# A hybrid decoder step: value chunks projected last, first head turned inside the last chunk, search opening in nine steps

## Time and profile before

| | before |
|---|---|
| median of three runs | 1811.48 us |
| profiled execution | 1811.48 us, its span 1810.0 us |
| PE busy | 1616.5 us, 89% of the span |
| DVE busy | 873.3 us, 48% |
| ACT busy | 679.2 us, 38% |
| POOL busy | 576.2 us, 32% |
| late projections, search, end of front | 218.9 to 535.5 us of the span |

### The profile page before, as it was taken

One profiled execution on the slowest core, in us unless ns is written; L12 is line 12 of the kernel. 1 busy time (PEld: TensorE's weight loads), 2 busy tenths in 40 slices (PEclk: granted clock), 3 DMA queues, 4 the chain that ended last, 5 costly groups with the idle time before them and its releaser, 6 DMA issues.

```text
span 1810.0 us, 29717 instructions
## 1 busy us (share of the span) xinstructions
PE 1616.5 (89%) x10786; PEld 1514.5 (84%) x10786; DVE 873.3 (48%) x1998; ACT 679.2 (38%) x1777; POOL 576.2 (32%) x715
## 2 busy tenths in 40 slices
PE   4696869899948889887699799999999999999998
PEld 3594669899847777775499699999999999999998
DVE  1904877877857888886521722312313303313214
ACT  4414647757427777874312421021121111111111
POOL 2344145624654343312112052142132232232310
PEclk7798989999979999998799999999999999999999
DMA  7700023353323121103530121111111111111002
GB/s 256 252 24 6 24 89 106 104 186 110 107 83 113 59 94 53 42 8 110 214 118 13 47 84 38 42 46 46 46 46 46 46 46 37 56 46 35 12 1 97
DMA packets 138045, 135.30 MB, mean 75 GB/s; under 512 B 7229, under 2 KB 126957, under 8 KB 137302
## 3 DMA queue, kind: packets, MB, share of 16 engines
q1 hardware_dynamic: 111190, 106.43, 18.4%
q10 hardware_dynamic: 25104, 24.64, 4.2%
q0 software_dynamic: 1648, 2.89, 0.5%
HBM read 115.29 MB, written 27.04 MB: 79 GB/s over the span
## 4 chain that ended last, share of the span: by engine, by line
PE 48%; DVE 2%; ACT 1%; DMA 1%; POOL 0%; issue 0%; DVEq 0%; SPq 0%; ACTq 0%
PE bank L2385 28%; PE wide L2401 14%; PE bank L2364 5%; PE wide L2348 1%; DVE xn L2616 0%; DVE alo L2626 0%; DVE rstd L2600 0%; DMA out_y_p<-yn 0%; DMA ow<-in_w_out 0%; ACT ahi L2501 0%; POOL owl L2532 0%; DVE yn L2670 0%; ACT gwh L2459 0%; PE bank L2425 0%; ACT L2473 0%; ACT L2491 0%
## 5 line engine op out<-in xcount | busy, mean ns | idle before, releaser
L2637 DVE TENSOR_TENSOR hf<-bank,sg 128x352 f32<-128x352 f32 x66 | 34.6, 525 | 464.6 <-PE bank L2385 455.4
L2546 POOL TENSOR_TENSOR hlo<-hf,hhi 128x352 fp32r<-128x352 f32 x66 | 62.6, 949 | 504.9 <-ACT hhi L2475 504.9
L2385 PE MATMUL bank<-ahi,gwh 128*128 128x352 f32 x1056 | 196.5, 328 | 11.2 <-DVE hf L2637 6.6
L2650 DVE SCALAR_TENSOR_TENSOR x<-wide,modT,x 128x352 f32<-128x352 f32 (+1 forms) x264 | 151.3, 573 | 96.8 <-PE wide L2401 96.8
L2385 PE MATMUL bank<-ahi,gwl 128*128 128x352 f32 x1056 | 194.1, 326 | 0.0
L2385 PE MATMUL bank<-alo,gwh 128*128 128x352 f32 x1056 | 192.2, 324 | 2.0 <-DVE alo L2626 2.0
L2385 PEld LDWEIGHTS bank<-ahi,gwh 128*128 128x128 f32 x1056 | 176.3, 190 | 14.1 <-DVE hf L2637 6.9
L2385 PEld LDWEIGHTS bank<-alo,gwh 128*128 128x128 f32 x1056 | 174.4, 189 | 2.7 <-DVE alo L2626 2.7
L2385 PEld LDWEIGHTS bank<-ahi,gwl 128*128 128x128 f32 x1056 | 176.6, 191 | 0.0
L2401 PE MATMUL wide<-hlo,dwh 128*128 128x352 f32 x528 | 171.3, 325 | 0.0
L2401 PE MATMUL wide<-hhi,dwl 128*128 128x352 f32 x528 | 170.4, 323 | 0.0
(11 more groups left out here) (347 smaller groups left out, 3473.1 us busy)
## 6 DMA issues: line engine op xcount, KB each, us to landing
gw<-in_w_gate_up SPq DMA_DIRECT2D x44, 512.0 KB, 4.9
raw<-in_w_ada ACTq DMA_DIRECT2D x14, 1024.0 KB, 8.6
dw<-in_w_down SPq DMA_DIRECT2D x22, 512.0 KB, 3.5
raw<-in_w_ada SPq DMA_DIRECT2D x10, 1024.0 KB, 7.5
raw<-in_w_in ACTq DMA_DIRECT2D x8, 1024.0 KB, 5.8
scr_x<-xT SPq DMA_DIRECT2D x1, 4224.0 KB, 18.3
xnat<-in_x_prompt SPq DMA_DIRECT2D x8, 512.0 KB, 5.3
scr_q<-ubuf SPq DMA_DIRECT2D x32, 128.0 KB
```

What stands on the lines that cost most here:

```text
L2385: mm = pe.matmul(pb[2 * s + side][:, 0:THIRD], a[r][:, k, side, :], b[:, k, third(th)], start=(p == 0 and k == 0), stop=(p == 2 and k == K ...
L2546: pool.tensor_tensor(hlo[:, r, third(th)], hf[:, (3 * r + th) % 2, :], hhi[:, r, third(th)].bitcast(F32), ALU.subtract).then_inc(h_lo, 1)
L2637: v.tensor_tensor(hf[:, s, :], pb[2 * s + 1][:, 0:THIRD], sg[:, s, :], ALU.mult).then_inc(h_mul, 1)
L2650: ins = v.scalar_tensor_tensor(out=x1[:, d, cols], in0=src[:, 0:n], scalar=modT[:, 40 + d, 0:1], in1=x1[:, d, cols], op0=ALU.mult, op1=ALU ...
```

## The change

`LATE` becomes qa, qa, ka, ka, kv, qb, qb, va, va: the values are projected last. The high and low parts of the first head's stacks are taken after unit 4 of chunk 8 and no longer after unit 6. PE turns one stack behind each of the units 6, 7 and 8 of chunk 8 (`turn_first_head`); ACT copies its half at the same unit, DVE still after the search. The opening of the search is nine steps instead of two, so 80 steps are dealt over the same 73 slots; seven slots hold two steps, and the bits' counts begin at the twelfth unit instead of the sixth. In the opening the two additions of the causal mask go over a step's tiles in turn. In `attention` ACT's `high_v(0)` moves to the head of the fourth round of its loop.

The diff, cut to its core:

```diff
@@ -290,21 +290,22 @@
...
-    NSTEPS = 2 + 2 * BITS + 2 + 7
+    OPENING = 9
+    NSTEPS = OPENING + 2 * BITS + 2 + 7
...
     for q in range(BITS):
-        tallies_after.setdefault(slot_of(1 + 2 * q) + 4, []).append(q)
+        tallies_after.setdefault(slot_of(OPENING - 1 + 2 * q) + 4, []).append(q)
...
     CH = [("iq", IQ, 256), ("iq", IQ + 256, 256), ("ik", PROJ - P, P)]
-    LATE = [("qa", QA, 256), ("qa", QA + 256, 256), ("ka", KA, 256), ("ka", KA + 256, 256), ("va", VA, 256),
-            ("va", VA + 256, 256), ("qb", QB, 256), ("qb", QB + 256, 256), ("kv", KB, 256)]
+    LATE = [("qa", QA, 256), ("qa", QA + 256, 256), ("ka", KA, 256), ("ka", KA + 256, 256), ("kv", KB, 256),
+            ("qb", QB, 256), ("qb", QB + 256, 256), ("va", VA, 256), ("va", VA + 256, 256)]
...
     LOAD_AT = 7
+    FIRST_SPLIT_AT = 4
+    FIRST_TURN_AT = 6
@@ -640,10 +643,23 @@
...
+                    if u >= len(units) - (NTILE + 1) + FIRST_TURN_AT:
+                        turn_first_head(t - FIRST_TURN_AT)
                     if u == NIDX:
...
+
+            def turn_first_head(y):
+                src = (S["qst"], S["kst"], S["lst"])[y]
+                pe.wait_ge(S["q_lo"] if y == 0 else S["k_lo"], 1)
+                for half in range(2):
+                    if y:
+                        pe.wait_ge(S["dve_out"] if half else S["act_out"], y)
+                    for j in range(4):
+                        mm = pe.transpose(bank[2 + half][:, j * P:(j + 1) * P],
+                                          src[:, 4 * half + j].rearrange("p a d -> p (a d)").bitcast(F32), ident[:])
+                    mm.then_inc(S["filled"], 1)
...
-            for x in range(6):
...
         @block.scalar
...
-                        if u == len(units) - 3:
+                        if u >= len(units) - (NTILE + 1) + FIRST_TURN_AT:
+                            y = t - FIRST_TURN_AT
+                            act.wait_ge(S["filled"], 2 * y + 1)
+                            act.activation((S["qS"], S["kH"], S["kL"])[y][0][:, 0:512], bank[2][:],
+                                           ACT.Copy).then_inc(S["act_out"], 1)
+                        if u == len(units) - (NTILE + 1) + FIRST_SPLIT_AT:
                             act.wait_ge(S["q_in"][0], 16)
...
                 ada_bias(a)
-            for x in (0, 2, 4):
-                act.wait_ge(S["filled"], x + 1)
-                act.activation((S["qS"], S["kH"], S["kL"])[x // 2][0][:, 0:512], bank[2][:],
...
-                    if u == len(units) - 3:
+                    if u == len(units) - (NTILE + 1) + FIRST_SPLIT_AT:
@@ -1296,13 +1300,14 @@
...
+
+            def count_positive(first, last):
                 joined()
-                for a, r, o, w in tiles():
+                for a, r, o, w in list(tiles())[first:last]:
                     link(v.tensor_scalar(junk[0:r, o:o + w], sco[0:r, o:o + w], 0.0, 0.0, ALU.is_ge, ALU.add,
                                          accum_out=cnt[0:r, a:a + 1]))
 
-            def orient():
-
+            def signs():
@@ -1315,20 +1320,22 @@
...
-                for a, r, o, w in tiles():
+
+            def orient(first, last):
...
-                joined()
-
-                for a, r, o, w in tiles():
-                    for rep in range(2):
+                for rep in range(2):
+                    joined()
+                    for a, r, o, w in list(tiles())[first:last]:
                         if a < 6:
                             d = sig[:, o + w - P:o + w]
                             link(v.tensor_tensor(d, d, causal[:], ALU.add))
                         else:
                             d = sig[0:r, o:o + w]
                             link(v.tensor_tensor(d, d, valid[:], ALU.add))
-                        joined()
-                v.memset(up[:], 0.0).then_inc(cand_ready, 1)
+                joined()
+                if last == 7:
+                    v.memset(up[:], 0.0).then_inc(cand_ready, 1)
@@ -1397,7 +1404,9 @@
...
-            steps += [causal_scores, orient]
+            steps += [causal_scores, lambda: count_positive(0, 3), lambda: count_positive(3, 5),
+                      lambda: count_positive(5, 7), signs, lambda: orient(0, 2), lambda: orient(2, 4),
+                      lambda: orient(4, 5), lambda: orient(5, 7)]
@@ -1433,9 +1442,9 @@
...
             joined()
-            for x in (1, 3, 5):
-                v.wait_ge(S["filled"], x + 1)
-                v.tensor_copy((S["qS"], S["kH"], S["kL"])[x // 2][0][:, 512:1024], bank[3][:]
+            for y in range(3):
+                v.wait_ge(S["filled"], 2 * y + 2)
+                v.tensor_copy((S["qS"], S["kH"], S["kL"])[y][0][:, 512:1024], bank[3][:]
                               ).then_inc(S["dve_out"], 1)
@@ -1868,9 +1877,10 @@
...
             act.wait_ge(zeroed, 1)
-            high_v(0)
             for n in range(LAST):
                 h, i = divmod(n, NTILE)
+                if n == 3:
+                    high_v(0)
```

More of the change, by code:

```diff
@@ L775, in _ @@
                 ada_turn(a)
-            for x in range(6):
-                src = (S["qst"], S["kst"], S["lst"])[x // 2]
-                if x < 2:
-                    pe.wait_ge(S["q_lo"], 1)
-                else:
-                    pe.wait_ge(S["k_lo"], 1)
-                if x >= 2:
-                    pe.wait_ge(S["dve_out"] if x % 2 else S["act_out"], x // 2)
-                for j in range(4):
-                    mm = pe.transpose(bank[2 + x % 2][:, j * P:(j + 1) * P],
-                                      src[:, 4 * (x % 2) + j].rearrange("p a d -> p (a d)").bitcast(F32), ident[:])
-                mm.then_inc(S["filled"], 1)
         @block.scalar
```

2 lines of the change are left out of this document (1 added, 1 removed).

## The result

The change makes the kernel faster: 1802.51 us as the median of seven runs (1797.77 to 1806.37), beside 1811.71 for the kernel before in the same series. The medians differ by 9.2 us. The ratio, estimated from these runs, is 0.9937, with an interval of 0.9923 to 0.9951, and stands for 11.4 us; the forecast was 17.1. The profiled execution after took 1800.94 us, its span 1799.4.

A forecast was written before the change was run, and what follows sets the result against it. The prediction saw four engines working as a chain, none saturated. Its steps put the engines' restart at 518.4 instead of 535.54, so 1811.48 - 17.1 = 1794.4 us; own range 1788 to 1800, 8-in-10 range 1782 to 1806.

The forecast's parts named there:

- rival B: Normed chunks become DVE's, each paying the whole 1.8 and more: 203 instead of 193.5, total 1804; chance 20 in 100.
- (a): Opening in nine steps: ACT no longer stands behind it, so PE's chunk 1 starts at 251.0, 14.0 earlier.
- Rival D: The opening gives only half, another wait holding PE for 7 us of the 14: 1801.4; chance 6 in 100.
- (b): Six normed chunks in a row, 1 to 6, take 193.5 in sum, so chunk 7 starts at 444.5; nine of fourteen given back.
- its waits of 6.6 are the cover: DVE's waits per normed chunk were to hide the 1.8 of extra bit steps, letting only 0.2 show.
- its sign, 35 a chunk: Profile sign in chunks 2, 3, 5 and 6: 35 each would mean rival B, 33 each the forecast.
- (c): The search's last decision, sharing its unit with its tally, comes 18.3 behind chunk 7's start, at 462.8.
- (d): The rest of DVE's search after the last decision takes 45.6, done at 508.4; ends 4.6 less or more.
- the rule on the shared port: DVE mask beside POOL's split, 4.55 before; the forecast allowed 4.6 either way for it, 1790 or 1795.
- (e): From DVE's end, copy, transposes, last unit and eight stores take 10.0; engines restart at 518.4, 17.1 earlier.
- (f): Moving `high_v(0)` in `attention` costs nothing, the values' load covering it; ends 1 gained, 3 lost.

The follow-up runs named there:

- e5: e3 with the same 80 steps dealt otherwise: one per slot through the sixth normed chunk, the other 20 beside the two value chunks; 1791.71 us, ratio 0.9886.
- e8: The kernel after the change with the search's four lowest bits left out, so it selects other keys; ratio 0.9869.
- e3: The kernel after the change, but ACT instead of DVE copies the second half of each turned stack too; 1795.65 us, ratio 0.9906.
- e9: The kernel after the change with the three turnings and ACT's copies behind all units of the last chunk, as before; 1794.26 us, ratio 0.9894.
- e1: The kernel before the change with only the search's opening divided into nine steps; 1807.48 us, ratio 0.9970.
- e2: The kernel after the change with the opening back in its two old steps; 1807.58 us, ratio 0.9966.
- e7: e3 with SPLIT_AT 3 instead of 4: ACT and POOL split the next chunk's weights one unit earlier; ratio 0.9984.
- e11: e3 with POOL's split of the next weights ahead of its rotation of unit 4, ACT's part unmoved; ratio 0.9981.
- e10: e3 with DVE's scale of the unit before ahead of the search's steps instead of behind them; 1795.79 us, ratio 0.9906.

## Why the prediction was right, and where its sum was off

The time lies in the range of 1782 to 1806, and the kernel became faster, as forecast. But 1802.51 is outside the forecast's own range of 1788 to 1800 and next to rival B's 1804, and the gain is little more than half of the 17.1. By its steps:

- (a) held to a tenth: chunk 1 at 250.71 (251.0 forecast), chunk 0 shorter by 13.95 (14.0), in eight kernels alike. Rival D is out.
- (b) failed in size. Chunks 1 to 6 took 196.53 instead of 193.5. That the sum came so near is partly luck: chunk by chunk the misses are +3.1, +2.0, -1.6, +0.4, -1.2 and +0.4. Two errors stand in it. The bare order was priced too high: with one step in a slot it is 189.80 (e5) or 188.98 (e8), where my sum without the allowance for the steps (0.7 in chunk 1, 0.2 in four others) was 192.0. The double slots were priced far too low: 1.5 in sum, and 7.5 measured (e5 and e8). The wrong sentence is "its waits of 6.6 are the cover". Of DVE's 23.6 of waits in these chunks of the kernel after, all but 1.5 stand in the first 14 us of a chunk; from 297.0 to 312.2 in chunk 2 there are next to none, and a step more that stands there, ahead of unit 4's scale, shows whole (2.90 and 2.45 between e3 and e5, where a step is 2.1). That is rival B's mechanism, at 1.3 a chunk on average instead of 1.8; its sign, 35 a chunk, shows in chunk 2 alone. It was given 20 in 100, and a good part of it came true.
- (c) 17.5 behind the start of chunk 7 (18.3), 464.73 (462.8) in all.
- (d) 47.7 instead of 45.6, with the error where the rule on the shared port was weighed. The timelines of POOL and DVE of the kernel after:

```profile
466.78 4.62 POOL L1034 TENSOR_TENSOR wlo<-raw,whi 128x2048 fp32r<-128x2048 f32 x1 [7.63 <-ACT whi L828]
...
467.91 3.50 DVE L1375 TENSOR_TENSOR kc<-cnt,kp 128x2 f32<-128x2 f32 x1
...
471.33 0.15 DVE L1376 TENSOR_TENSOR up<-up,cand 128x2 f32<-128x2 f32 x1
...
496.89 3.23 POOL L1125 TENSOR_TENSOR lst<-kn,kst 128x1024 fp32r<-128x1024 f32 x1
...
495.88 2.00 DVE L1398 SCALAR_TENSOR_TENSOR sig<-sig,kp,selE 128x896 f32<-128x896 f32 x1
...
497.91 3.16 DVE L1401 SCALAR_TENSOR_TENSOR sig<-selG,sig 128x896 f32<-128x896 f32 x1
```

`kc`, an instruction on two columns, takes 3.50 and ends with the split, where the next one of its form takes 0.15; two selections with two inputs take 2.00 and 3.16 beside the subtractions of the stacks, where the wider tile's take 1.28 and 1.23. e5 has the same three without POOL beside them: `kc` comes at 477.8, when the split has ended at 474.78, and takes 0.16, and the two selections take 1.15 and 1.09. Together that is about 6.3 lost, where the one mask before lost some 4.2. The Trainium skill (SBUF — State Buffer, "Who interferes with whom") says that a DVE instruction with two inputs in SBUF contends with a GpSimd instruction that reads SBUF; the trace agrees, with these rows. My reading that the split would stand beside counting steps and block nothing was wrong by one small instruction of two inputs that came just then.
- (e) held, 9.5 for 10.0, by the row of events named, and e3 shows it by taking it away. But I priced it as a given, and compared it only with the old end: e9 shows that the same change without the early turning has 4.8 there.
- (f) nothing that can be told, as forecast: PE's first transpose of the next head comes 9.0 to 9.7 behind the restart in the kernels with the move, 9.3 and 9.7 in the two without (before and e1).

To the restart the forecast was 3.5 off (518.4 and 521.92). Behind it the profiled execution lost 3.1 more, 2.5 of it ahead of the load of `ow`: in `sample_attention` PE waits 3.2 for the load of `vw`, and 0.9 before. e1, with the old code there, waits 2.3 for it and has the longest stretch of all, and e9, with the new code, waits 0.9, so an effect of the change is not shown. The median then lies 1.6 over the profiled run, and the runs lie between 1797.8 and 1806.4, a width that the two disturbed columns of the table (4.3 and 3.5) can make.

How the gain is shared out I judged wrongly before the experiments: I expected all but the opening to pay only 2 to 3 (e2) and the opening 11 to 12 (e1), and they pay 6.2 and 5.4, alike within the noise. The opening's 14 loses 7 by the restart, and the rest of the change, at a price of 7.3 in the chunks, takes 12.9 off the end, although the early turnings in it lose.

Open stays by which link a step more shows in the chunk: that DVE has next to no waits in the middle is seen, which way leads from its lateness, or from ACT's tallies, to PE is not shown, since moving the split (e7, e11) or the scale (e10) did not free it. The two additions of the causal mask, the earlier parts of the stacks and the move of `high_v(0)` were not run alone.

The best kernels of the study keep the change's opening and order, and either take DVE out of the turning or turn behind all units: e3 at 0.9906, e9 at 0.9894, and e5, e3 with the steps dealt unevenly, at 0.9886 (1791.71 us), which these runs don't tell apart.

## What to carry to other kernels

Idle time of an engine covers more work only if it stands at the place where the work is put: look at where in the period the waits lie, not at their sum. When a piece of work is moved ahead of others on an in-order engine, ask what it waits for at its new place; here a turning of 1 us carried the wait for a whole search ahead of the last unit. And a change of several parts should be priced one part at a time against the best form of the others, since a part that loses can hide in a sum that gains.

## What the runs showed of the hardware that was not expected

A tiny DVE instruction beside a long POOL one can last until that one ends: `kc` on 128x2 took 3.50, and the two ended within 0.01 (471.41 and 471.40). And the same code in front of chunk 0 takes between 218.2 and 222.5 in fourteen profiles, with a stretch of 354.6 to 358.1 behind the restart, so that a single profile of this kernel tells the total only to some 4 us.
